# Two of eight query heads multiplied as one product of 512 columns, and the last head's tiles in banks of their own

## The chip, the cores and the metric

The kernel runs on one core of one Trainium2 chip. The metric is device time in microseconds (us) of one execution, the median of several runs. The core's engines are TensorE (PE, with its weight loads listed apart as PEld), VectorE (DVE), ScalarE (ACT), GpSimd (POOL) and SyncE (SP), which here only issues DMAs. Each engine works through its own instructions in order and waits on semaphores for the others.

## What is computed

The reference is two transformer blocks over 256 tokens of width 1024. Each block ends in a "product key" expert layer; the change touches only the first step of that layer, the queries, in both blocks:

```
q = (xb @ w_q).reshape(B, T, PEER_HEADS, 2, PEER_DKEY // 2)     # 8 heads, two halves of 128
s1 = jnp.einsum('bthd,nd->bthn', q[..., 0, :], k1)              # 128 keys for each half
s2 = jnp.einsum('bthd,nd->bthn', q[..., 1, :], k2)
v1, i1 = lax.top_k(s1, PEER_TOPK); v2, i2 = lax.top_k(s2, PEER_TOPK)
...                                                             # 16 of 256 candidates per head,
u_sel = jnp.take(u_tab, idx, axis=0)                            # then the chosen experts
h = jnp.einsum('bthkd,btd->bthk', u_sel, xb)
```

The kernel multiplies by all 16384 experts and masks with gates, rather than gathering.

## The kernel before

**Weights.** All weight matrices pass through one ring of four slots of 128 x 1024 floats. SyncE loads a slot, ScalarE rounds it to `whi` (the type fp32r), and GpSimd (in some stages VectorE) writes the rest `wlo = ring - whi`. The other operand is split in the same way. A product of a weight tile and the operand is then made of three products: `whi` by the rounded operand, `whi` by its rest, `wlo` by the rounded operand. The kernel calls this `split_product` (lines 732 to 734), and each of its matmuls has 256 columns (the 256 tokens).

**The query stage** (function `experts` of each engine, loop over heads `h`). The operand is `R = (rhi, rlo)`, the residual's rounded part and rest. A head has two weight tiles (`c` = 0, 1), one for each half of the query. Function `tile` runs 8 chunks of 128 rows for each, with three matmuls a chunk. Both tiles of a head lie side by side in one PSUM bank, 4 or 5 by turns. The order on TensorE is: the tiles of head `h`, then the scores of head `h - 1` (line 1235), which read the query from `qT`, a buffer of two places in SBUF (`h % 2`). ScalarE copies each head's bank to `qT` when both tiles are done (line 1689, semaphore `q_copied`), then rounds two weight slots (line 1677), then copies the scores of the head before to `scores` (lines 1698 and 1699, semaphore `s_copied`).

**VectorE in this stage.** It first finishes the normed activations in banks 0 to 3 (`normed`), then walks over the heads: `normed_lows` at `h == 1` (line 1941, semaphore `xl_ready`), and for each head and each half of the tokens (`t` = 0, 1) the two levels of `top16` (lines 2252 to 2264, and line 2290 between them). From head 3 on it also adds pairs of expert results: `add_pair`, line 2276, which waits for a copy by ScalarE (line 1705).

**The expert rounds** follow on TensorE: each tile is 8 chunks of one matmul of 512 columns, `whi` by both parts of the normed activations (`hboth`, line 1259), and one of 256 columns, `wlo` by the rounded part (line 1260). Banks 2, 3 and 0, 1 take them. The half of a bank that holds `whi` by the rest is copied out by ScalarE, and VectorE adds the other half.

Of the kernel before, what the change touches and what calls it, by code (L numbers as in the profile page):

```python
# [22 lines left out]
P = 128  # L23
F32 = mybir.dt.float32
F16 = mybir.dt.float16
F32R = mybir.dt.float32r
U32 = mybir.dt.uint32
ALU = mybir.AluOpType
ACT = mybir.ActivationFunctionType
# [3 lines left out]
S = 256  # L33
TT = S // P
KC = D // P
EPS = 1e-6

HEADS = 8
# [10 lines left out]
RING = 4  # L49
# [22 lines left out]
HALF = NKEY // 2  # L72
HALF_ROUND = ROUNDS // 2
U_EXP, U_MID = 12, 13
FIRST_ADD_HEAD = 3
WARM_UP = 9
V_LOGITS = 22
# [44 lines left out]
RAW_AT = 22528  # L122
# [97 lines left out]
def block_program(nc, weights, const1, const2, gains, keys_in, x, out):  # L220
    with ExitStack() as ctx:
# [3 lines left out]
        def over_at(name, base, at, shape, dt=F32):  # L225

            return nc.alloc_sbuf_tensor_at(name, shape, dt, offset=offset_of[base] + at)
# [13 lines left out]
        whi = sb("whi", [P, RING, SLOT], F32R)  # L241
        wlo = sb("wlo", [P, RING, SLOT], F32R)
        act = placed("act", [P, NKEY, S])
# [11 lines left out]
        ps = ctx.enter_context(nc.psum_tensor("ps", [P, 8, 512], F32))  # L255
# [3 lines left out]
        qT = work[:, 2048:3072].rearrange("p (b c t) -> p b c t", b=2, c=2)  # L259
# [55 lines left out]
        start = TT * D  # L315
# [72 lines left out]

        late_scores = carve(LATE_SCORES, 4, TT, 2 * NKEY)[0].rearrange("p b t (c k) -> p b t c k", c=2)

        rhi = over_at("rhi", "act", 4 * RAW_AT, [P, KC, S], F32R)
        rlo = over_at("rlo", "act", 4 * (RAW_AT + KC * S), [P, KC, S], F32R)

        def scores_of(h):

# [18 lines left out]
        lo_ready = [sem(f"lo_ready{j}") for j in range(RING)]  # L414
        left_ready = sem("left_ready")
        sb_left = sem("sb_left_ready")
        slot_used = sem("slot_used")
# [24 lines left out]
        xl_ready = sem("normed_lows_ready")  # L442
# [71 lines left out]
        peer = []  # L514
        for b in (1, 2):
            peer.append({n: sem(f"peer{b}_{n}") for n in (
                "q_copied", "s_ready", "s_copied",
                "gelu_done", "sums_ready", "exp_ready", "sel_ready", "selT_ready", "rows_ready", "eq_ready", "hot_ready",
                "u_low", "u_added", "gates_ready", "gates_used", "shi_ready", "pair_ready", "acc_ready", "done")})
        fin_ready = sem("final_ready")  # L520
# [11 lines left out]
        def bank(i, a=0, b=512):  # L532
            return ps[:, i, a:b]
# [161 lines left out]
        def _(pe):  # L695
# [493 lines left out]
            def experts(b, keys):  # L1189
                n = peer[b]  # L1190
                first_q, first_u, first_v = FIRST[f"q{b + 1}"], FIRST[f"u{b + 1}"], FIRST[f"v{b + 1}"]

                def tile(j, dst, x=(hhi, hlo), kcs=range(KC), start=True):

                    for kc in kcs:
                        c = slice(kc * P, (kc + 1) * P)
                        mm = split_product(dst, (whi[:, j, c], wlo[:, j, c]), (x[0][:, kc, :], x[1][:, kc, :]),
                                           start and kc == 0, kc == KC - 1)
                    if kcs[-1] == KC - 1:
                        mm.then_inc(slot_used, 1)  # L1200

                R = (rhi, rlo)
# [10 lines left out]
                pe.wait_ge(left_ready, left + 4)  # L1213
                for c in range(2):
                    tile(c, bank(4, c * S, (c + 1) * S), R, range(4, 8))
                for h in range(1, HEADS + 1):
                    if h < HEADS:
                        for c in range(2):
                            pe.wait_ge(lo_ready[(2 * h + c) % RING], (first_q + 2 * h + c) // RING + 1)
                            if h >= 2 and c == 0:  # L1220
                                pe.wait_ge(n["q_copied"], h - 1)
                            tile((2 * h + c) % RING, bank(4 + h % 2, c * S, (c + 1) * S), R, range(4 if h + c == 1 else 0, KC))
                            if h + c == 1:
                                scale_turns(2 * b + 1)
                    if h:
                        g = h - 1
                        pe.wait_ge(n["q_copied"], g + 1)
                        if g == 1:
                            pe.wait_ge(xn_ready, 4 * b + 4)
                        if g >= 2:  # L1230
                            pe.wait_ge(n["s_copied"], g - 1)
                        for t in range(TT):
                            for c in range(2):
                                kT = keys[:, c if b == 0 else 2 * g + c, :]
                                mm = pe.matmul(bank(6 + g % 2, (2 * t + c) * P, (2 * t + c + 1) * P),  # L1235
                                               qT[:, g % 2, c, t * P:(t + 1) * P], kT, start=True, stop=True)
                        mm.then_inc(n["s_ready"], 1)
# [44 lines left out]
                for w in range(3):  # L1282
                    for t in range(TT):
                        mm = pe.transpose(bank(4 + w // 2, (w % 2) * S + t * P, (w % 2) * S + (t + 1) * P),
                                          esel[:, t, w, :, :].rearrange("p h k -> p (h k)"), ident[:, :])
# [121 lines left out]
        def _(eng):  # L1407
# [261 lines left out]
            def experts(b):  # L1669
                n = peer[b]  # L1670
# [8 lines left out]
                for h in range(HEADS + 1):  # L1679
                    if h == 2:  # L1680
                        for c in range(4):
                            eng.wait_ge(xn_ready, 4 * b + c + 1)
                            eng.activation(hhi[:, 2 * c:2 * c + 2, :], bank(c).rearrange("p (j t) -> p j t", j=2), ACT.Copy)\
                               .then_inc(xh_ready, 1)
                    if h < HEADS:
                        eng.wait_ge(slot_used, first_q + 2 * h + 2)
                        if h >= 2:
                            eng.wait_ge(n["s_ready"], h - 1)
                        eng.activation(qT[:, h % 2, :, :], bank(4 + h % 2).rearrange("p (c t) -> p c t", c=2), ACT.Copy)\
                           .then_inc(n["q_copied"], 1)  # L1690
                        for c in range(2):
                            high(first_q + 2 * h + c + RING, (2 * h + c) % RING)
                    if h:
                        eng.wait_ge(n["s_ready"], h)
                        if h == 1:
                            eng.wait_ge(nrec, NORM_AT[2 * b + 1] + 1)
                        out = bank(6 + (h - 1) % 2).rearrange("p (t c k) -> p t c k", t=TT, c=2)
                        eng.activation(scores_of(h - 1)[:, 0], out[:, 0], ACT.Copy, scale=token_scale(0))
                        eng.activation(scores_of(h - 1)[:, 1], out[:, 1], ACT.Copy, scale=token_scale(1))\
                           .then_inc(n["s_copied"], 1)  # L1700
# [175 lines left out]
        def _(eng):  # L1876
# [50 lines left out]
            def normed(k):  # L1927

                take_scale(k)
                for b in range(4):  # L1930
                    for c in (2 * b, 2 * b + 1):
                        x = bank(b, c % 2 * S, (c % 2 + 1) * S)
                        last = eng.scalar_tensor_tensor(x, x, gcol[:, k, c:c + 1], scale_row, ALU.mult, ALU.mult)
                    last.then_inc(xn_ready, 1)
# [332 lines left out]
            def experts(b):  # L2267
                n = peer[b]
                first_v = FIRST[f"v{b + 1}"]

                def add_pair(p):

                    eng.wait_ge(n["u_low"], p + 1)
                    bb = BESIDE_BANK[p % 2]
                    a = act[:, 2 * p:2 * p + 2, :]
                    eng.tensor_tensor(a, ps[:, bb:bb + 2, 0:S], a, ALU.add).then_inc(n["u_added"], 1)  # L2276

                normed(2 * b + 1)
                for h in range(HEADS):
                    if h == 1:  # L2280
                        normed_lows(b)
                    eng.wait_ge(n["s_copied"], h + 1)
                    early = 3 * (h - FIRST_ADD_HEAD)
                    for t in range(TT):
                        mid = (lambda: add_pair(early + 1)) if h >= FIRST_ADD_HEAD and t == 1 else None
                        top16([scores_of(h)[:, t, c, :] for c in range(2)], [cand[:, 2, c * NKEY:(c + 1) * NKEY] for c in range(2)],
                              [val[:, c, :] for c in range(2)], [idx[:, t, h, c, :] for c in range(2)], between=mid)

                        s = cand[:, 0, :]
                        last = eng.tensor_tensor(s.rearrange("p (a b) -> p a b", a=TOPK), over(val[:, 0, :], TOPK),  # L2290
                                                 val[:, 1:2, :].to_broadcast([P, TOPK, TOPK]), ALU.add)
                        settle(last)
                        if h >= FIRST_ADD_HEAD and t == 0:
                            add_pair(early)
                        top16([s], [cand[:, 1, :]], [top[:, t, h, :]], [pos[:, t, h, :]])
                        if h >= FIRST_ADD_HEAD and t == 1:
                            add_pair(early + 2)
# [338 lines left out]
```

## Time and profile before

| | |
|---|---|
| median of 3 runs | 1984.44 us (1984.0 to 1984.62) |
| the profiled execution's own time | 1984.3 us |
| its span in the trace | 1982.5 us, 1.8 us less than its time |
| TensorE busy | 1974.8 us, 100% |
| GpSimd, VectorE, ScalarE busy | 1429.7, 1281.9, 1042.3 us |
| mean granted TensorE clock | 0.999 |

Times in rows are microseconds from the span's start unless they are in a column of mean nanoseconds. A matmul's listed duration overlaps with those of its neighbours, since they are pipelined; the distance between two starts is what one of them takes of the engine's time. A "waits" view lists only idle time with what ended it. The chain of work lists, for the work that ended last, each piece on it.

### The profile page before, as it was taken

The numbers are of one execution on the slowest core, as the hardware profiler recorded it, in microseconds if no ns is written. First come the engines' busy times: TensorE is split into PE (matmuls) and PEld (weight loads), VectorE is DVE, ScalarE is ACT, GpSimd is POOL, SyncE is SP. The second block draws the span as 40 slices with busy tenths as digits, with TensorE's granted clock in tenths as the row PEclk, the third lists the DMA queues.
The fourth block names the chain that finished last, engine by engine and source line by source line (L and its number), as shares of the span: only waits on it lengthen the run. The fifth ranks groups of instructions, "written<-read, shape, count | busy, mean of one in ns | idle before, by whom it ended". The sixth has DMA issues, their size and how long they took to land.

```text
span 1982.5 us, 39083 instructions
## 1 busy us (share of the span) xinstructions
PE 1974.8 (100%) x13990; PEld 1766.6 (89%) x13990; DVE 1281.9 (65%) x2178; ACT 1042.3 (53%) x1361; POOL 1429.7 (72%) x606
## 2 busy tenths in 40 slices
PE   9999999999999999999999999999999999999998
PEld 9899898888888888888889899888888888888887
DVE  5256387864766899953336738886467789994333
ACT  6556545565555544445447665556555554444444
POOL 6667878888777878854448757888877787884442
PEclk9999999999999999999999999999999999999999
DMA  8444545555555555566655345555555555555653
GB/s 273 161 139 149 179 161 186 188 183 190 177 170 175 174 169 171 177 208 206 195 186 178 123 144 166 192 187 186 182 176 172 172 178 169 175 174 181 201 190 127
DMA packets 100467, 351.44 MB, mean 177 GB/s; under 512 B 12464, under 2 KB 15408, under 8 KB 100272
## 3 DMA queue, kind: packets, MB, share of 16 engines
q1 hardware_dynamic: 99680, 348.61, 53.2%
q10 hardware_dynamic: 720, 1.92, 0.3%
q8 instruction: 44, 0.72, 0.1%
q14 instruction: 23, 0.19, 0.0%
HBM read 349.44 MB, written 1.05 MB: 177 GB/s over the span
## 4 chain that ended last, share of the span: by engine, by line
PE 99%; DMA 0%; DVE 0%; ACT 0%; POOL 0%; SPq 0%; issue 0%
PE ps L1259 24%; PE ps L1325 12%; PE ps L1260 12%; PE ps L1327 12%; PE ps L1328 6%; PE ps L1326 6%; PE ps L732 4%; PE ps L734 4%; PE ps L733 4%; PE ps L889 4%; PE ps L1251 3%; PE ps L891 2%; PE ps L816 1%; PE ps L1235 1%; PE ps L1137 1%; PE ps L926 1%
## 5 line engine op out<-in xcount | busy, mean ns | idle before, releaser
L653 POOL TENSOR_TENSOR wlo<-ring,whi 128x1024 fp32r<-128x1024 f32 x567 | 1375.2, 2431 | 511.3 <-ACT whi L1677 425.8
L1677 ACT ACTIVATE whi<-ring 128x1024 fp32r<-128x1024 f32 x536 | 566.5, 1060 | 718.2 <-PE ps L1328 387.2
L1259 PE MATMUL ps<-hboth,whi 128*128 128x512 f32 x2048 | 714.6, 395 | 0.0
L1260 PE MATMUL ps<-hboth,wlo 128*128 128x256 f32 x2048 | 567.7, 277 | 0.0
L1259 PEld LDWEIGHTS ps<-hboth,whi 128*128 128x128 f32 x2048 | 384.1, 188 | 87.2
L1325 PE MATMUL ps<-whi,shi 128*128 128x512 f32 x1024 | 404.2, 395 | 0.0
L1327 PE MATMUL ps<-wlo,shi 128*128 128x512 f32 x1024 | 400.4, 391 | 0.0
L1260 PEld LDWEIGHTS ps<-hboth,wlo 128*128 128x128 f32 x2048 | 384.7, 188 | 0.0
L1328 PE MATMUL ps<-whi,slo 128*128 128x256 f32 x1024 | 286.7, 280 | 0.0
L1326 PE MATMUL ps<-whi,slo 128*128 128x256 f32 x1024 | 285.7, 279 | 0.0
L1327 PEld LDWEIGHTS ps<-wlo,shi 128*128 128x128 f32 x1024 | 192.2, 188 | 43.4
L1325 PEld LDWEIGHTS ps<-whi,shi 128*128 128x128 f32 x1024 | 192.4, 188 | 40.3
L2405 DVE TENSOR_TENSOR wlo<-ring,whi 128x1024 fp32r<-128x1024 f32 x64 | 78.7, 1230 | 230.6 <-ACT whi L1677 230.6
L2399 DVE TENSOR_TENSOR slo<-act,shi 128x512 fp32r<-128x512 f32 x128 | 181.9, 1421 | 23.6 <-ACT shi L1739 23.6
L1326 PEld LDWEIGHTS ps<-whi,slo 128*128 128x128 f32 x1024 | 192.3, 188 | 0.0
L1328 PEld LDWEIGHTS ps<-whi,slo 128*128 128x128 f32 x1024 | 192.2, 188 | 0.0
L2358 DVE TENSOR_TENSOR work<-iota,ps 128x1024 f16<-128x1024 f16 x128 | 155.1, 1211 | 0.0
L1446 ACT ACTIVATE whi<-ring 128x1024 fp32r<-128x1024 f32 x105 | 108.0, 1053 | 76.4 <-PE ps L891 35.9
L2368 DVE TENSOR_TENSOR act<-ps,act 128x512 f32 (+1 forms) x128 | 87.0, 682 | 37.9 <-PE ps L1251 32.9
L2276 DVE TENSOR_TENSOR act<-ps,act 128x512 f32<-128x512 f32 x64 | 44.3, 692 | 103.1 <-ACT act L1705 103.0
L2376 DVE TENSOR_TENSOR act<-ps,act 128x512 f32 (+1 forms) x64 | 44.2, 691 | 78.1 <-ACT act L1705 78.1
L732 PE MATMUL ps<-hboth,whi 128*128 128x256 f32 x328 | 94.5, 288 | 0.0
(332 smaller groups left out, 2905.2 us busy)
## 6 DMA issues: line engine op xcount, KB each, us to landing
ring<-in_weights SPq DMA_DIRECT2D x651, 512.0 KB, 3.3
act<-in_const SPq DMA_DIRECT2D x11, 198.0 KB, 4.0
act<-in_const SPq DMA_DIRECT2D x8, 192.0 KB, 4.5
xres<-in_x SPq DMA_DIRECT2D x4, 256.0 KB, 4.9
act<-in_keys ACTq DMA_DIRECT2D x1, 1024.0 KB, 4.7
ring<-in_weights SPq DMA_DIRECT2D x2, 256.0 KB, 4.8
act<-in_fgain ACTq DMA_DIRECT2D x1, 512.0 KB, 3.4
out<-act SPq DMA_DIRECT2D x1, 512.0 KB, 2.6
```

Of the source, the lines that this page charges most:

```text
L653: pool.tensor_tensor(wlo[:, j, :], ring[:, j, :], whi[:, j, :].bitcast(F32), ALU.subtract)\
L732: pe.matmul(dst, wide[0], narrow[0], start=start, stop=False, skip_group_check=True)
L1259: pe.matmul(bank(b), whi[:, j, c], hboth[:, :, kc, :], start=kc == 0, stop=False, skip_group_check=True)
L1260: mm = pe.matmul(bank(b, 0, S), wlo[:, j, c], hhi[:, kc, :], start=False, stop=kc == KC - 1, skip_group_check=True)
L1325: pe.matmul(bank(b), high, whi[:, j, o:o + 512], start=start, stop=False, skip_group_check=True)
L1326: pe.matmul(bank(b, 0, 256), low, whi[:, j, o:o + 256], start=False, stop=stop, skip_group_check=True)
L1327: pe.matmul(bank(b), high, wlo[:, j, o:o + 512], start=False, stop=False, skip_group_check=True)
L1328: return pe.matmul(bank(b, 256, 512), low, whi[:, j, o + 256:o + 512], start=False, stop=stop, skip_group_check=True)
L1446: eng.activation(whi[:, m % RING, :], ring[:, m % RING, :], ACT.Copy).then_inc(hi_ready[m % RING], 1)
L1677: eng.activation(whi[:, j, :], ring[:, j, :], ACT.Copy).then_inc(hi_ready[j], 1)
L2358: eng.tensor_tensor(hot2[:, j], iota[:, :].unsqueeze(1).to_broadcast([P, TOK, NKEY]), over(row(1, at), NKEY), ALU.is_equal)
L2399: eng.tensor_tensor(slo[:, j, :, :], act[:, bass.ds(p * 2, 2), :], shi[:, j, :, :].bitcast(F32), ALU.subtract)\
```

## The change

For heads 5 and 6 a new function `joined_tile` does what the expert rounds do: one matmul of 512 columns, `whi` by `rboth` (which is `rhi` and `rlo` as one tensor at the same addresses), and one of 256 columns, `wlo` by `rhi`. Their banks are 2 and 3 for head 5, and 0 and 1 for head 6 (`JOINED_BANK`). Because those banks hold the normed activations before, TensorE waits for `xl_ready` first. The query now lies in two halves of a bank: ScalarE copies the one to `qT` (semaphore `q_low`), and VectorE adds the other to it (`join_query`, semaphore `q_joined`), at head 2 of its loop, once before each half of the tokens. TensorE's scores of heads 5 and 6 wait for `q_joined`. The last head's two tiles go to banks 5 and 4, half of each, and ScalarE copies each half by itself as soon as its tile is done.

```diff
-        rhi = over_at("rhi", "act", 4 * RAW_AT, [P, KC, S], F32R)
-        rlo = over_at("rlo", "act", 4 * (RAW_AT + KC * S), [P, KC, S], F32R)
+        rboth = over_at("rboth", "act", 4 * RAW_AT, [P, 2, KC, S], F32R)
+        rhi, rlo = rboth[:, 0], rboth[:, 1]
...
+                def joined_tile(j, b):
+
+                    for kc in range(KC):
+                        c = slice(kc * P, (kc + 1) * P)
+                        pe.matmul(bank(b), whi[:, j, c], rboth[:, :, kc, :], start=kc == 0, stop=False, skip_group_check=True)
+                        mm = pe.matmul(bank(b, 0, S), wlo[:, j, c], rhi[:, kc, :], start=False, stop=kc == KC - 1,
+                                       skip_group_check=True)
+                    mm.then_inc(slot_used, 1)
+
+                def query_there(g):
+
+                    if g in JOINED_BANK:
+                        pe.wait_ge(n["q_joined"], list(JOINED_BANK).index(g) + 1)
+                    else:
+                        pe.wait_ge(n["q_copied"], g + 1 if g < min(JOINED_BANK) else g + 1 - len(JOINED_BANK))
+
                 for h in range(1, HEADS + 1):
-                    if h < HEADS:
+                    if h in JOINED_BANK:
+                        pe.wait_ge(xl_ready, 4 * b + 4)
+                        for c in range(2):
+                            pe.wait_ge(lo_ready[(2 * h + c) % RING], (first_q + 2 * h + c) // RING + 1)
+                            joined_tile((2 * h + c) % RING, JOINED_BANK[h] + c)
+                    elif h < HEADS:
...
-                            tile((2 * h + c) % RING, bank(4 + h % 2, c * S, (c + 1) * S), R, range(4 if h + c == 1 else 0, KC))
+                            dst = bank(5 - c, 0, S) if h == HEADS - 1 else bank(4 + h % 2, c * S, (c + 1) * S)
+                            tile((2 * h + c) % RING, dst, R, range(4 if h + c == 1 else 0, KC))
...
-                        pe.wait_ge(n["q_copied"], g + 1)
+                        query_there(g)
...
+                        if h in JOINED_BANK:
+                            eng.activation(qT[:, h % 2, :, :], ps[:, JOINED_BANK[h]:JOINED_BANK[h] + 2, S:2 * S], ACT.Copy)\
+                               .then_inc(n["q_low"], 1)
...
+                        else:
+                            for c in range(2):
+                                eng.wait_ge(slot_used, first_q + 2 * h + c + 1)
+                                last = eng.activation(qT[:, h % 2, c, :], bank(5 - c, 0, S), ACT.Copy)
+                            last.then_inc(n["q_copied"], 1)
...
+                def join_query(h):
+
+                    bb = JOINED_BANK[h]
+                    eng.wait_ge(n["q_low"], list(JOINED_BANK).index(h) + 1)
+                    eng.tensor_tensor(qT[:, h % 2, :, :], ps[:, bb:bb + 2, 0:S], qT[:, h % 2, :, :], ALU.add).then_inc(n["q_joined"], 1)
+
...
+                        if h == 2:
+                            join_query(5 + t)
```

On TensorE, at the border between heads 4 and 5 of the first block, the instructions of the kernel before are these (line 1235 the scores of head 3, then head 5's first tile):

```order
L1235 MATMUL ps<-act,work 128x128 [waits peer1_s_copied,peer1_q_copied]
L1235 MATMUL ps<-act,work 128x128 x3
L732 MATMUL ps<-rhi,whi 128x256 [waits peer1_q_copied,lo_ready2]
L733 MATMUL ps<-rlo,whi 128x256
L734 MATMUL ps<-rhi,wlo 128x256
L732 MATMUL ps<-rhi,whi 128x256
```

At the same place of the changed kernel, with its own line numbers (`normed_lows_ready` is the name of `xl_ready`):

```order
L1259 MATMUL ps<-act,work 128x128 [waits peer1_s_copied,peer1_q_copied]
L1259 MATMUL ps<-act,work 128x128 x3
L1222 MATMUL ps<-rboth,whi 128x512 [waits lo_ready2,normed_lows_ready]
L1223 MATMUL ps<-rboth,wlo 128x256
L1222 MATMUL ps<-rboth,whi 128x512
L1223 MATMUL ps<-rboth,wlo 128x256
```

Two matmuls stand for three, and the first of them waits for VectorE's `normed_lows`. A little further, between heads 6 and 7, the changed kernel has this:

```order
L1223 MATMUL ps<-rboth,wlo 128x256
L1259 MATMUL ps<-act,work 128x128 [waits peer1_s_copied,peer1_q_joined]
L1259 MATMUL ps<-act,work 128x128 x3
L733 MATMUL ps<-rboth,whi 128x256 [waits peer1_q_copied,lo_ready2]
L734 MATMUL ps<-rboth,whi 128x256
```

The scores of head 5 stand behind head 6's tiles as before, but wait for VectorE instead of ScalarE. On VectorE, where head 2 begins in the first block, the kernel before has:

```order
L2264 MAX_INDEX work<-val,work 128x8 [waits dve_step]
L2252 MAX val<-work 128x8 [waits peer1_s_copied,dve_step]
L2252 MAX val<-work 128x8
L2255 MAX_INDEX work<-val,work 128x8 [waits dve_step]
L2256 MATCH_REPLACE work<-val,work 128x128
```

and the changed kernel:

```order
L2298 MAX_INDEX work<-val,work 128x8 [waits dve_step]
L2316 TENSOR_TENSOR work<-ps,work 128x512 [waits peer1_q_low,peer1_s_copied,dve_step]
L2286 MAX val<-work 128x8 x2
L2289 MAX_INDEX work<-val,work 128x8 [waits dve_step]
L2290 MATCH_REPLACE work<-val,work 128x128
```

One addition of 512 elements stands ahead of head 2's first `MAX`; a second one stands ahead of the second half of its tokens.

## Rows read from the trace of the kernel before

**Rows 1.** The profile's page, part 1: busy time of each engine

```profile
PE 1974.8 (100%) x13990; PEld 1766.6 (89%) x13990; DVE 1281.9 (65%) x2178; ACT 1042.3 (53%) x1361; POOL 1429.7 (72%) x606
```

**Rows 2.** Waits of TensorE in the whole span: total us, times, longest

```profile
PE ps L1394 <- DVE work L2466: 1.1, 1, 1.1
PE ps L816 <- DVE wlo L2472: 0.3, 1, 0.3
```

**Rows 3.** Chain of work, first block's query stage: start us, us, what

```profile
284.13 0.89 PE ps L1235 x8
...
290.77 0.89 PE ps L1235 x8
...
297.42 1.85 PE ps L1235 x16
```

**Rows 4.** Windows: length, busy us (instructions) of PE, PEld, DVE, ACT, POOL; clock, DMA, GB/s

```profile
284.13:290.78 6.65, 6.65 (x58) 6.65 (x58) 6.30 (x27) 3.22 (x5) 4.76 (x2) 1.00 0.48 168
305.37:310.91 5.54, 5.54 (x33) 4.84 (x33) 3.63 (x14) 2.61 (x3) 4.98 (x3) 1.00 0.63 204
```

**Rows 5.** Timeline of ScalarE in the expert rounds: start us, us, [idle before]

```profile
313.73 1.06 ACT L1677 ACTIVATE whi<-ring 128x1024 fp32r<-128x1024 f32 x1 [0.62 <-PE ps L1260]
...
413.57 1.06 ACT L1677 ACTIVATE whi<-ring 128x1024 fp32r<-128x1024 f32 x1 [0.71 <-PE ps L1260]
```

**Rows 6.** Timeline of TensorE, query tile: start us, us, line, operands

```profile
285.22 0.28 PE L732 MATMUL ps<-rhi,whi 128*128 128x256 f32 x1
285.33 0.28 PE L733 MATMUL ps<-rlo,whi 128*128 128x256 f32 x1
285.45 0.28 PE L734 MATMUL ps<-rhi,wlo 128*128 128x256 f32 x1
```

**Rows 7.** Timeline of TensorE, expert tile

```profile
305.21 0.39 PE L1259 MATMUL ps<-hboth,whi 128*128 128x512 f32 x1
305.44 0.27 PE L1260 MATMUL ps<-hboth,wlo 128*128 128x256 f32 x1
305.55 0.40 PE L1259 MATMUL ps<-hboth,whi 128*128 128x512 f32 x1
```

**Rows 8.** Timeline of TensorE, output projection with 512 and 256 columns

```profile
224.70 0.40 PE L889 MATMUL ps<-whi,mhi 128*128 128x512 f32 x1
...
235.31 1.03 PE L700 MATMUL ps<-ident,xres 128*128 128x128 f32 x8
```

**Rows 9.** Timeline of ScalarE, copies of heads 5 and 6

```profile
284.17 0.60 ACT L1689 ACTIVATE work<-ps 128x512 f32<-128x512 f32 x1 [3.43 <-PE ps L734]
...
290.81 0.60 ACT L1689 ACTIVATE work<-ps 128x512 f32<-128x512 f32 x1 [3.43 <-PE ps L734]
```

**Rows 10.** Timeline of VectorE, first block: low halves, heads 1 to 3

```profile
273.30 2.48 DVE L1941 TENSOR_TENSOR hboth<-ps,hboth 128x512 fp32r<-128x512 f32 x4
...
278.57 0.43 DVE L2290 TENSOR_TENSOR work<-val 128x256 f32<-128x256 f32 x1
...
287.11 0.49 DVE L2252 MAX8 val<-work 128x8 f32<-128x128 f32 x2
...
293.24 0.49 DVE L2252 MAX8 val<-work 128x8 f32<-128x128 f32 x2
...
302.76 1.37 DVE L2290 TENSOR_TENSOR work<-val 128x256 f32<-128x256 f32 x1
307.11 0.69 DVE L2276 TENSOR_TENSOR act<-ps,act 128x512 f32<-128x512 f32 x1 [2.97 <-ACT act L1705]
```

**Rows 11.** Timeline of VectorE, second block: head 2's second half, first add

```profile
1226.08 0.49 DVE L2252 MAX8 val<-work 128x8 f32<-128x128 f32 x2
...
1239.94 0.69 DVE L2276 TENSOR_TENSOR act<-ps,act 128x512 f32<-128x512 f32 x1 [2.96 <-ACT act L1705]
```

**Rows 12.** Chain of work, second block's last scores

```profile
1230.25 1.85 PE ps L1235 x16
```

**Rows 13.** Timeline of GpSimd, one head's cycle

```profile
285.79 4.76 POOL L653 TENSOR_TENSOR wlo<-ring,whi 128x1024 fp32r<-128x1024 f32 x2 [1.88 <-ACT whi L1677]
```

More of the change, by code:

```diff
@@ L74 @@
 U_EXP, U_MID = 12, 13
+JOINED_BANK = {5: 2, 6: 0}
 FIRST_ADD_HEAD = 3
@@ L516, in block_program @@
             peer.append({n: sem(f"peer{b}_{n}") for n in (
-                "q_copied", "s_ready", "s_copied",
+                "q_copied", "q_low", "q_joined", "s_ready", "s_copied",
                 "gelu_done", "sums_ready", "exp_ready", "sel_ready", "selT_ready", "rows_ready", "eq_ready", "hot_ready",
@@ L1220, in experts @@
                             if h >= 2 and c == 0:
-                                pe.wait_ge(n["q_copied"], h - 1)
-                            tile((2 * h + c) % RING, bank(4 + h % 2, c * S, (c + 1) * S), R, range(4 if h + c == 1 else 0, KC))
+                                pe.wait_ge(n["q_copied"], h - 1 if h < HEADS - 1 else min(JOINED_BANK))
+                            dst = bank(5 - c, 0, S) if h == HEADS - 1 else bank(4 + h % 2, c * S, (c + 1) * S)
+                            tile((2 * h + c) % RING, dst, R, range(4 if h + c == 1 else 0, KC))
                             if h + c == 1:
@@ L1685, in experts @@
                     if h < HEADS:
-                        eng.wait_ge(slot_used, first_q + 2 * h + 2)
+                        if h < HEADS - 1:
+                            eng.wait_ge(slot_used, first_q + 2 * h + 2)
                         if h >= 2:
                             eng.wait_ge(n["s_ready"], h - 1)
-                        eng.activation(qT[:, h % 2, :, :], bank(4 + h % 2).rearrange("p (c t) -> p c t", c=2), ACT.Copy)\
-                           .then_inc(n["q_copied"], 1)
+                        if h in JOINED_BANK:
+                            eng.activation(qT[:, h % 2, :, :], ps[:, JOINED_BANK[h]:JOINED_BANK[h] + 2, S:2 * S], ACT.Copy)\
+                               .then_inc(n["q_low"], 1)
+                        elif h < HEADS - 1:
+                            eng.activation(qT[:, h % 2, :, :], bank(4 + h % 2).rearrange("p (c t) -> p c t", c=2), ACT.Copy)\
+                               .then_inc(n["q_copied"], 1)
+                        else:
[3 more added lines that the diff above has]
+                            last.then_inc(n["q_copied"], 1)
                         for c in range(2):
```

## The prediction

> **What bounds the kernel now.** I read the page's busy times first: TensorE is busy 1974.8 of 1982.5 us, the next engine 1429.7 [rows 1]. A share of the whole span can hide waits, so I asked for TensorE's waits. There are two in the whole execution, 1.1 and 0.3 us, both near the start and neither in the stage of the change [rows 2]. The chain of work says the same of the query stages: one piece of TensorE follows another, with nothing between [rows 3, 12]. So each nanosecond that TensorE's own stream gets shorter there comes off the end, and a wait put before it is paid in full.
>
> The question is then what TensorE's stream costs. Listed durations can't be summed: a query tile's matmuls are listed with 0.28 us, but start 0.11 to 0.12 us apart [rows 6]. The reader should use distances between starts.
>
> **The cost of a tile, old form.** The scores of two neighbouring heads start at 284.13, 290.77 and 297.42: a head takes 6.645 us, of which its scores take 0.89 [rows 3]. The rest is two tiles, 2.878 us each; with 24 matmuls a tile that is 119.9 ns a matmul and 360 ns a chunk.
>
> **The cost of a tile, new form.** The expert rounds already run exactly the new pair, 512 columns of `whi` by both parts and 256 of `wlo`. Two of ScalarE's roundings, each released by a tile's end, stand at 313.73 and 413.57, with 36 tiles between [rows 5]: 2.773 us a tile, 347 ns a chunk. The timeline shows how: the 512 start takes 0.23 us, the 256 start 0.11 to 0.12 [rows 7]. Columns streamed stay at 768 a chunk; what goes is about 13 ns for each matmul left out.
>
> **TensorE's sum.** Two heads of two tiles in each of two blocks are 8 tiles: 8 x (2.878 - 2.773) = 0.84 us less. The operand and the place differ from the expert rounds, so I bound the new pair. In the output projection, pairs of 512 and 256 columns go from 224.70 to 235.31, 30 of them [rows 8]: 354 ns each, 6 ns less than the old chunk, or 0.4 us less in 64 chunks. On the other side, the last two heads' scores together take 1.85 us, not twice 0.89 [rows 3, 12]. Should that 0.07 be the wait for the last head's copy, the split copy could give 2 x 0.07 back, so the gain is 0.4 to 1.0 us. I take 0.84, since those rows have the same shapes, the same order and the same weight slots. I take nothing for the split copy: ScalarE's copy takes 0.60 us [rows 9], and the scores of head 6 cover it with their 0.89.
>
> A sentence on the notes: the Trainium skill, page "TensorE: Matmul & The Clock Gate", section "Wait — 56ns, not 53.3ns?", puts a fixed cost of about 2.5 ns on each matmul beyond its columns. By that, 64 fewer would give an estimated 0.16 us, against 0.84 from the rows. The rows show 12 to 13 ns a matmul, and the measurement decides.
>
> **The waits that are added, in TensorE's time.** Each is checked for how early its releaser is.
> - Head 5 waits for `xl_ready`. The low halves start at 273.30 and take 2.48, ending 275.8 [rows 10]. Head 5 begins one head and the scores before 284.13 + 0.89: at 285.02 - 6.645 = 278.4. That is 2.6 us early. Head 6 asks for nothing more.
> - Head 5's scores wait for the first join, where they stood at 290.77 [rows 3]; with four shorter tiles they come at 290.35. ScalarE's copy begins at 284.17 and takes 0.60 [rows 9], so it is done at 284.8 or earlier. VectorE comes to head 2 at 287.11 and so finds it done. An addition of this shape out of PSUM takes 0.69 [rows 10]; it ends at 287.8, 2.5 us early.
> - Head 6's scores wait for the second join, at 297.42 - 0.42 = 297.0. ScalarE's part is done by 291.4 [rows 9]. VectorE's second half of head 2 stood at 293.24 and is one join later, 293.93; this join ends at 294.6, 2.4 us early. In the second block the same numbers are 1226.08 + 2 x 0.69 = 1227.5 against 1230.25 - 0.42 = 1229.8, 2.4 us early [rows 11, 12].
>
> **VectorE's extra work**, two joins of 0.69 a block, is 1.4 us. What is queued behind them is heads 2 to 7, and then the first `add_pair`, for which TensorE's later rounds wait. Before that first addition VectorE sits idle 2.97 us in the first block and 2.96 in the second, waiting for ScalarE [rows 10, 11]. The 1.4 us go in there, and even with ScalarE's release 0.4 us sooner some 1.1 us of idle time is left. If that cover were gone, the rest would be carried down the queue, and TensorE has more slack in its banks before it waits. So: nothing.
>
> **ScalarE, GpSimd and the loads.** ScalarE's copies for heads 5 and 6 are as long as before; for the last head one of 512 columns becomes two of 256, the first in time in which it sat 3.43 us idle each head [rows 9]. GpSimd splits a head's two tiles in 4.76 us and then idles 1.88 [rows 13]; a head 0.21 shorter leaves 1.67. DMA is busy 0.48 in a head's cycle and 0.63 in the expert rounds, which run at the new pace already [rows 4]. Nothing.
>
> **Sum.** 1984.3 - 0.84 = 1983.5 by the profiled execution, which was 0.14 under the median of the three runs. By the median it is 1983.6, my forecast.
>
> **The rivals.**
> - *The gain is lost in the columns.* What is streamed is the same 768 columns; the pace of the output projection's pairs, or one still nearer the old chunk, leaves 0 to 0.4 us: about 1984.3. For it: those 354 ns [rows 8]. Against: the same shapes in the expert rounds.
> - *Weight loads set the pace.* In the head's cycle the load unit is busy 6.65 of 6.65 us, in the expert rounds 4.84 of 5.54 [rows 4]. If a load and not the columns filled each slot, leaving 64 out would save 64 x 120 ns = 7.7 us: 1976.7, faster by 0.4%. Against: a 512-column matmul would then start its follower after 0.12 us, and it does so after 0.23 [rows 7]. The Trainium skill, page "TensorE: Matmul & The Clock Gate", section "Back-to-back issue gap", lets load and matmul set the distance together and gives 131 ns for 512 columns; no such short distance is in these rows. Chance 2 in 100.
> - *A join comes late.* TensorE stands still while VectorE is in its top-16 work. The addition between its two levels takes 0.43 to 1.37 us from one half to another [rows 10]; were five of them ahead of the second join 0.65 longer each, that join would be 3.25 later, 0.8 beyond the slack of 2.4, in each block. That is 1984.44 - 0.84 + 1.6 = 1985.2. It decides, slower than before, from 2.4 + 0.42 = 2.8 us of lateness in each block, and passes 0.2% (4 us, about the least that a measurement of this kernel can tell from no change) from 4.8 us. For it: VectorE is 6.30 of 6.65 us busy there [rows 4]. Against: both blocks show the same slack.
>
> **How the numbers follow.** The forecast has 0.80 (its own range 1983.0 to 1984.2), the lost gain 0.11, weight loads 0.02, a late join 0.05, of which 0.02 is beyond 0.2%; 0.02 is left for what I don't see, on both sides. The range goes from the full 1.0 us off the lowest runs (1984.0 - 1.0 = 1983.0) less 0.4 for their scatter, 1982.6, up to the late join, 1985.2. Faster by over 0.2%: 0.03; slower: 0.03; within: 0.94.
>
> **What would show it.** Right: new tiles 2.77 us apart, the two heads' cycles 6.44 instead of 6.645, 64 matmuls fewer, TensorE's waits still two; VectorE idle before its first `add_pair` shrunk from 2.97 to about 1.1. Wrong: a wait of TensorE's scores for VectorE's join, or of head 5's first matmul for the low halves; new tiles at 2.88; or head cycles near 5 us.

## The result, and the profile after

The changed kernel takes 1988.97 us in the median of 13 runs (1988.47 to 1990.29), against 1984.45 us of the kernel before (13 runs): a ratio of 1.0023, 95% interval 1.0016 to 1.0031. That is 4.5 us slower, where 0.84 us faster was forecast. Its profiled execution took 1989.01 us with a span of 1987.2, 4.7 us over the span before. Two single executions on record stand far outside all others and count in no ratio: 3255 us of the kernel before (beside e1 to e4) and 6940 us of e2; nothing on record says why.

I first checked the stage that the change touches. The chain of work of the changed kernel, at the places of [rows 3] (line 1259 is the scores, 1235 before):

```profile
277.44 0.89 PE ps L1259 x8
...
283.98 0.89 PE ps L1259 x8
...
290.42 0.89 PE ps L1259 x8
...
297.06 1.78 PE ps L1259 x16
```

Head 5 takes 6.54 us and head 6 takes 6.44, against 6.645. The last scores take 1.78 instead of 1.85. Together that is 0.38 us a block, 0.76 in both, close to the forecast. The trace has 64 matmuls fewer, 13926 against 13990, as forecast. TensorE's waits, the whole answer, answer to [rows 2]: none was added.

```profile
PE ps L1418 <- DVE work L2508: 1.1, 1, 1.1
PE ps L817 <- DVE wlo L2514: 0.4, 1, 0.4
```

VectorE's timeline has the two joins (line 2316) and then the first `add_pair` (line 2310), which answers to the last row of [rows 10]:

```profile
287.07 0.69 DVE L2316 TENSOR_TENSOR work<-ps,work 128x512 f32<-128x512 f32 x1
...
293.37 0.69 DVE L2316 TENSOR_TENSOR work<-ps,work 128x512 f32<-128x512 f32 x1
...
306.79 0.69 DVE L2310 TENSOR_TENSOR act<-ps,act 128x512 f32<-128x512 f32 x1 [3.24 <-ACT act L1739]
```

The joins are on time, and VectorE still idles 3.24 us before its first addition. That is not the 1.1 us that was forecast: the two joins did go into its queue, but its own additions between the two levels of `top16` were shorter by more than that. Of three such additions from 289 us on, the kernel before has 0.85, 1.37 and 1.37 us, the changed one 0.42, 0.42 and 0.99. The second of them, before and after:

```profile
296.12 1.37 DVE L2290 TENSOR_TENSOR work<-val 128x256 f32<-128x256 f32 x1
```

```profile
296.84 0.42 DVE L2332 TENSOR_TENSOR work<-val 128x256 f32<-128x256 f32 x1
```

Why their length varies no run here shows. The query stage did what was asked of it. The loss is behind it, in code that the change doesn't touch. ScalarE's roundings in the expert rounds, each released by a tile's end, answer to [rows 5]:

```profile
313.56 1.06 ACT L1701 ACTIVATE whi<-ring 128x1024 fp32r<-128x1024 f32 x1 [0.68 <-PE ps L1284]
...
415.32 1.06 ACT L1701 ACTIVATE whi<-ring 128x1024 fp32r<-128x1024 f32 x1 [0.77 <-PE ps L1284]
```

Again 36 tiles lie between, but they take 2.827 us each instead of 2.773. TensorE's timeline of such a tile shows where, beside [rows 7] (1283 and 1284 are the lines 1259 and 1260 before):

```profile
305.11 0.28 PE L1284 MATMUL ps<-hboth,wlo 128*128 128x256 f32 x1
305.23 0.40 PE L1283 MATMUL ps<-hboth,whi 128*128 128x512 f32 x1
305.47 0.28 PE L1284 MATMUL ps<-hboth,wlo 128*128 128x256 f32 x1
305.59 0.40 PE L1283 MATMUL ps<-hboth,whi 128*128 128x512 f32 x1
305.83 0.28 PE L1284 MATMUL ps<-hboth,wlo 128*128 128x256 f32 x1
305.94 0.40 PE L1283 MATMUL ps<-hboth,whi 128*128 128x512 f32 x1
306.17 0.28 PE L1284 MATMUL ps<-hboth,wlo 128*128 128x256 f32 x1
306.29 0.40 PE L1283 MATMUL ps<-hboth,whi 128*128 128x512 f32 x1
```

Three chunks go from 305.23 to 306.29, 353 ns each. In the kernel before, two chunks go from 305.21 to this row, 693 ns by the unrounded starts, 347 each:

```profile
305.90 0.39 PE L1259 MATMUL ps<-hboth,whi 128*128 128x512 f32 x1
```

Nobody waits; the same instructions are simply spaced a little wider. How long this lasts is best seen by counting instructions in windows of equal length. First the kernel before, then the changed one; the first number behind the window is its length, the next TensorE's busy time with its matmuls in brackets, then that of its weight loads:

```profile
320.00:431.00 111.00, 111.00 (x642) 97.10 (x641) 91.97 (x245) 62.59 (x81) 96.53 (x41) 1.00 0.57 189
450.00:475.00 25.00, 25.00 (x146) 22.05 (x145) 9.30 (x13) 14.57 (x19) 21.75 (x10) 1.00 0.58 191
500.00:620.00 120.00, 120.00 (x955) 105.13 (x954) 83.87 (x119) 61.92 (x80) 95.09 (x41) 1.00 0.52 173
1260.00:1371.00 111.00, 111.00 (x642) 97.01 (x641) 90.43 (x233) 64.55 (x83) 95.21 (x40) 1.00 0.58 189
```

```profile
320.00:431.00 111.00, 111.00 (x630) 96.30 (x629) 90.13 (x242) 61.22 (x80) 94.12 (x40) 1.00 0.55 184
450.00:475.00 25.00, 25.00 (x147) 21.86 (x146) 8.61 (x12) 13.61 (x18) 21.95 (x10) 1.00 0.61 198
500.00:620.00 120.00, 120.00 (x954) 105.09 (x953) 84.39 (x119) 61.53 (x80) 96.28 (x40) 1.00 0.52 174
1260.00:1371.00 111.00, 111.00 (x630) 96.22 (x629) 90.70 (x235) 61.16 (x78) 94.47 (x40) 1.00 0.56 187
```

The slower pace fills rounds 0 to 12 of both blocks (642 against 630 matmuls) and is gone behind them, where the program has six transposes of the gate rows between the tiles. The granted clock is 1.00 in all of these windows. The 52 tiles cost 52 x (2.827 - 2.773) = 2.8 us more a block, 5.6 in both. With the 0.76 gained this makes +4.8 us, and the span grew by 4.7.

In what follows, "fast pace" is 347 ns a chunk of one 512- and one 256-column matmul, "slow pace" 353 to 354.

### The profile page after: what moved, and what is told of

It is laid out like the page before. It is cut to its first block, busy times and chain, and to the rows that moved or that the text cites. A ratio compares the mean times of both kernels' runs of the same rounds, so it can differ in the third digit from the quotient of the medians.

```text
span 1987.2 us, 38963 instructions
## 1 busy us (share of the span) xinstructions
PE 1979.4 (100%) x13926; PEld 1766.0 (89%) x13926; DVE 1281.1 (64%) x2182; ACT 1042.6 (52%) x1363; POOL 1428.7 (72%) x606
## 4 chain that ended last, share of the span: by engine, by line
PE 99%; DMA 0%; DVE 0%; ACT 0%; POOL 0%; SPq 0%; issue 0%
PE ps L1283 24%; PE ps L1284 12%; PE ps L1349 12%; PE ps L1351 12%; PE ps L1352 6%; PE ps L1350 6%; PE ps L733 4%; PE ps L735 4%; PE ps L734 4%; PE ps L890 4%; PE ps L1275 3%; PE ps L892 2%; PE ps L817 1%; PE ps L1222 1%; PE ps L1259 1%; PE ps L1138 1%
```

## The experiments

What differs where the rounds begin is small. In the kernel before, the last two heads' scores take 1.85 us in the chain [rows 3, 12]: TensorE waits for ScalarE's copy of the last head, and one distance between starts is 175 ns instead of 112. In the changed kernel the split copy is there in time and the wait is gone. My theory was that this "lost wait" had set the pace; the rival was that the joined heads or their banks did.

**e1: the changed kernel with one copy.** The last head as before, heads 5 and 6 joined.

```diff
-                            dst = bank(5 - c, 0, S) if h == HEADS - 1 else bank(4 + h % 2, c * S, (c + 1) * S)
+                            dst = bank(4 + h % 2, c * S, (c + 1) * S)
...
-                            for c in range(2):
-                                eng.wait_ge(slot_used, first_q + 2 * h + c + 1)
-                                last = eng.activation(qT[:, h % 2, c, :], bank(5 - c, 0, S), ACT.Copy)
...
```

> The changed kernel with the last head as before: both tiles in one bank, one copy by ScalarE. Heads 5 and 6 stay joined. In the changed kernel's trace the first 13 expert rounds of each block (52 tiles) run at 353.6 ns a chunk against 346.7 before, 2 x 52 x 8 x 6.9 ns = 5.7 us, and the short wait in the last two heads' scores (a 9th start 175 ns behind the 8th, against 112) is gone. Theory 'lost wait': that wait put TensorE's stream into the fast pace. Here it is back, the rounds run at 346.7 again, and the kernel takes 1984.45 - 0.6 = 1983.8 us. Rival 'joined heads': the new products or their banks set the slow pace, and the kernel stays at about 1989.1 us.

1984.15 us, ratio 1.0002 (0.9992 to 1.0011). Its chain has the wait again, and its first window the old count:

```profile
297.04 1.85 PE ps L1259 x16
```

```profile
320.00:431.00 111.00, 111.00 (x642) 97.02 (x641) 91.97 (x243) 62.54 (x80) 96.49 (x41) 1.00 0.56 189
```

The joined heads alone don't make the slow pace. The 0.35 us over the expected 1983.8 may come from a short slow stretch: in the profiled execution, of 1984.36 us, rounds 13 to 15 of the second block and the first tile of round 16 ran at 353 ns, 13 tiles or 0.7 us. One of its ten executions took 1988.48 us; I return to this at e13.

**e2: the kernel before with the last head split only.** The same lines the other way round, no joined heads, and one more wait so that bank 4 is free for the second tile.

```diff
+                            if h == HEADS - 1 and c == 1:
+                                pe.wait_ge(n["q_copied"], h)
+                            dst = bank(5 - c, 0, S) if h == HEADS - 1 else bank(4 + h % 2, c * S, (c + 1) * S)
...
+                            for c in range(2):
+                                eng.wait_ge(slot_used, first_q + 2 * h + c + 1)
+                                last = eng.activation(qT[:, h % 2, c, :], bank(5 - c, 0, S), ACT.Copy)
...
```

> The kernel before with only the last head changed: its two tiles in banks 5 and 4, copied one by one; no joined heads. Theory 'lost wait': the scores' wait goes, the 52 tiles run at 353.6 ns a chunk, and the kernel takes 1984.45 + 5.7 - 0.14 = 1990.0 us. Rival 'joined heads': nothing changes the pace, 1984.3 us.

1989.72 us in the median of 8 runs, ratio 1.0027 (1.0016 to 1.0038): the whole loss, from the part of the change for which I had booked nothing.

```profile
297.14 1.78 PE ps L1238 x16
```

```profile
320.00:431.00 111.00, 111.00 (x630) 96.19 (x629) 90.18 (x242) 61.23 (x80) 94.11 (x41) 1.00 0.54 184
```

**e3: two banks, both copies late.**

```diff
-                                eng.wait_ge(slot_used, first_q + 2 * h + c + 1)
+                                eng.wait_ge(slot_used, first_q + 2 * h + 2)
```

> The changed kernel, but ScalarE's two copies of the last head both wait for the second tile; the banks stay 5 and 4. The second copy then ends about 0.66 us after the tile, against 0.60 for the one copy before. Theory 'lost wait': TensorE's scores wait again, somewhat over 63 ns, and the pace is fast: 1983.9 us. If any wait does it, that holds whatever its length; if the length matters (a phase), the pace can stay slow. Rival 'banks of the last head': slow, 1989 us.

1984.14 us, 0.9999 (0.9989 to 1.0009). The scores take 1.97 us, so the wait is about three times as long, and the pace is fast. The banks of the last head are not the cause. Nor is the layout of TensorE's program: its instructions are those of the changed kernel to the last one, and only ScalarE's copy comes later.

**e4: 18 small matmuls instead of 16.** Between the scores and the first expert tile stand 16 fp16 matmuls of 64 columns, whose results nobody reads; two more shift that tile by 60 ns without any wait.

```diff
-                for _ in range(2 * TOK):
+                for _ in range(2 * TOK + 2):
```

> The changed kernel with 18 instead of 16 small fp16 matmuls between the scores and the first expert tile (30 ns each, together 60 ns, as long as the lost wait). If the slow pace is a matter of when the first expert matmul starts in some rhythm, shifting it by 60 ns gives the fast pace back, 1983.9 us. If it takes an empty queue, a wait, to reset, the pace stays slow: 1989.1 us.

1983.77 us, 0.9998 (0.9988 to 1.0008), 642 matmuls in the first window. So the wait as such is not needed either. What counts is when, or in what state, the stream is entered; I call an entry the place where the expert tiles' matmuls begin or go on behind something else. "Lost wait" was half a theory: it fits this change and fails as a rule.

**e5, e6: 17 and 20 of them.** The same line with + 1 and + 4.

> The changed kernel with 17 small fp16 matmuls ahead of the first expert tile instead of 16; with 18 the fast pace was back. Theory 'rhythm': the pace hangs on when the first expert matmul starts within some rhythm, and 30 ns later is a third place in it; either pace is possible, 1984.0 or 1989.0 us, and nothing between. Rival 'load ahead': more time for the weight loads to run ahead is what helps, and 17 lie between 16 (slow) and 18 (fast).

> The changed kernel with 20 small fp16 matmuls. Theory 'rhythm': 120 ns later than with 16; the pace may be slow again, 1989.2 us, if the rhythm has come round. Rival 'load ahead' (more time ahead of the first expert tile helps): fast as with 18, 1984.0 us. A slow pace here would rule the rival out; a fast one leaves both open.

1983.42 us (0.9997, 0.9987 to 1.0006) and 1983.71 us (0.9997, 0.9988 to 1.0007), both fast. They left the rival "more time ahead is what helps" open.

**e7: the kernel before with 18.** The line of e4 in the kernel before.

> The kernel before, with 18 small fp16 matmuls instead of 16: its wait of 63 ns in the last scores and 60 ns of dummies on top. Theory 'rhythm': this is a further place, 123 ns behind the slow one; the same answer as with 20 dummies in the changed kernel. 1984.5 us if fast, 1990 us if slow. Rival 'any delay resets': fast.

1989.05 us, 1.0025 (1.0015 to 1.0035). This was a surprise in its place. The windows:

```profile
320.00:431.00 111.00, 111.00 (x642) 97.88 (x641) 91.97 (x245) 62.60 (x81) 96.61 (x41) 1.00 0.56 189
450.00:475.00 25.00, 25.00 (x143) 21.69 (x142) 9.06 (x13) 14.54 (x19) 21.18 (x10) 1.00 0.58 190
500.00:620.00 120.00, 120.00 (x942) 104.31 (x941) 83.07 (x118) 60.42 (x77) 94.02 (x40) 1.00 0.50 169
```

Rounds 0 to 12 are fast. The pace turns slow at the next entry, behind the transposes, nearly 150 us after the two added matmuls, and stays so through the rounds with gates (942 matmuls against 955). So a shift of 60 ns can decide the pace at a later entry. Something of it can be seen already before that entry: with the same 642 matmuls in the first window, the weight loads are busy 97.88 us instead of the 97.10 of the kernel before. I return to this behind e12.

**e8: a break after the first round.** 16 more such matmuls, into bank 4, between round 0 and the loop of the changed kernel.

```diff
                 beside_round(0, first=True)
+                for _ in range(2 * TOK):
+                    pe.matmul(bank(4, 0, HALF), iota[:, :], iota[:, 0:HALF], start=True, stop=True)
                 with pe.Fori(1, U_MID) as k:
```

> The changed kernel with 16 further small fp16 matmuls (into bank 4) after the first expert round, ahead of the loop. Theory 'the pace, once taken, lasts until the stream is broken': the four tiles of round 0 stay slow (353.6 ns a chunk), and the break gives a new draw; if it is fast, 48 tiles in each block run at 346.7 and the kernel takes 1989.0 - 2 x 48 x 8 x 0.0069 + 2 x 0.5 for the dummies = 1984.7 us. Rival 'the slow pace comes from something in these rounds other than how they are entered' (VectorE's or ScalarE's work beside them, the joined banks): the rounds stay slow, 1990 us.

1984.96 us, 1.0004 (0.9995 to 1.0014), 0.3 from what was expected. The first window has 643 matmuls; only round 0 stays slow:

```profile
320.00:431.00 111.00, 111.00 (x643) 97.10 (x642) 91.98 (x246) 62.59 (x81) 96.54 (x41) 1.00 0.56 190
```

This shows that a break can end the slow pace, and that what runs beside these rounds (VectorE, ScalarE, the loads) doesn't by itself keep it up.

**e9 to e12: 15, 14, 12 and 1 of them.** The line of e4 with - 1, - 2, - 4 and - 15, in the changed kernel.

> The changed kernel with 15 small fp16 matmuls ahead of the first expert tile. So far 16 without a wait is slow and everything with more time ahead of that tile (17, 18, 20 matmuls, or a wait of 63 ns or more) is fast in the 52 tiles. Theory 'rhythm': the entry hits one of a few places, so less time ahead can be fast as well; with 15, 14, 12 and 1 at least one of the four should be, 1983.7 us. Rival 'load ahead': too little time is what makes them slow, so 15 and fewer are all slow, 1989 us.

> The changed kernel with 14 small fp16 matmuls, 59 ns less ahead of the first expert tile. 'Rhythm': fast or slow, 1983.6 or 1989 us. 'Load ahead': slow, 1989 us.

> The changed kernel with 12 small fp16 matmuls, 117 ns less. 'Rhythm': fast or slow, 1983.5 or 1989 us. 'Load ahead': slow, 1989 us.

> The changed kernel with a single small fp16 matmul ahead of the first expert tile, 436 ns less. 'Rhythm': fast or slow, 1983.1 or 1988.6 us. 'Load ahead': slow, 1988.6 us. If 15, 14, 12 are fast and this one is slow, a number of small matmuls is needed to break the rhythm of what went before.

| kernel, small matmuls | us (median) | ratio to before, 95% | slow tiles in the profiled execution |
|---|---|---|---|
| changed, 15 (e9) | 1992.87 (4 runs) | 1.0043 (1.0027 to 1.0060) | 180: first block rounds 0 to 31, second 0 to 12 |
| changed, 14 (e10) | 1987.94 | 1.0020 (1.0010 to 1.0029) | 89: first block rounds 13 to 31, second 13 to the first tile of 16 |
| changed, 12 (e11) | 1983.39 | 0.9995 (0.9986 to 1.0005) | none |
| changed, 1 (e12) | 1982.48 | 0.9992 (0.9982 to 1.0001) | none |

The last column is from distances between 512-column starts in the trace (353 ns against 347). The slow tiles account for the times. With 0.054 us for each, and 0.029 us for each small matmul in each block, e9 should be 1983.5 - 0.1 + 9.7 = 1993.1 us and e10 1983.5 - 0.1 + 4.8 = 1988.2, within 0.3 of what was measured; 1983.5 is about what e4, e5 and e6 leave for 16 at the fast pace. The changed kernel itself has 104 slow tiles, which gives 1989.1 us. 12 and 1 are fast with less time ahead than the slow 16, so "more time ahead" falls. The windows of e9, the slowest kernel here, are slow in all four places:

```profile
320.00:431.00 111.00, 111.00 (x630) 96.19 (x629) 90.06 (x241) 61.22 (x80) 94.34 (x40) 1.00 0.55 184
450.00:475.00 25.00, 25.00 (x143) 21.68 (x143) 8.60 (x12) 13.23 (x17) 21.35 (x10) 1.00 0.58 188
500.00:620.00 120.00, 120.00 (x941) 104.20 (x941) 81.70 (x117) 61.88 (x80) 93.45 (x39) 1.00 0.51 170
1260.00:1371.00 111.00, 111.00 (x630) 96.32 (x629) 90.13 (x238) 61.47 (x79) 94.46 (x40) 1.00 0.56 187
```

**What precedes a slow entry behind the transposes.** The 16 traces, two blocks each, have 32 stretches of rounds 0 to 12. The fast ones come in two kinds, told apart by the weight loads' busy time in the window. The second block of e7 and that of e1 are of the rarer kind:

```profile
1260.00:1371.00 111.00, 111.00 (x642) 97.88 (x641) 91.82 (x237) 62.60 (x81) 96.60 (x41) 1.00 0.56 189
```

```profile
1260.00:1371.00 111.00, 111.00 (x642) 97.86 (x641) 89.89 (x228) 64.97 (x83) 94.54 (x40) 1.00 0.56 189
```

Five stretches have 97.86 to 97.88 us (both blocks of e7 and e10, the second of e1), and all five are slow behind the transposes. Nineteen have 96.99 to 97.10, and none of them is. Of the eight slow stretches one stays slow there, the first of e9. So an entry is hardly a fresh draw: what it brings went with the pattern in which the stream ran before. This was read from the traces afterwards, and no run was made to test it.

A break doesn't always end the slow pace either. From round 16 on, 32 small matmuls for the gates stand in each round. In the first block of e7, e9 and e10 the slow pace went on across all 16 of these breaks, and in the second block of e1, e7 and e10 it ended at the first.

**e13, e14: one small matmul in both kernels, side by side.**

> The kernel before with a single small fp16 matmul ahead of the first expert tile instead of 16: 2 x 0.44 us of dummies less. If all expert rounds run at 346.7 ns a chunk: 1984.3 - 0.9 = 1983.4 us. If this entry falls on the slow pace somewhere, 3 to 9 us more, and then it tells nothing of the change's own gain.

> The changed kernel with a single small fp16 matmul, as e12, beside e13 on the same chip. Theory 'the local sum was right': 0.8 us under e13 where both run at the fast pace throughout, 1982.5 us, and 1.7 us under the kernel before, outside its interval. Rival 'no gain of its own': the same as e13, 1983.4 us.

e13: 1983.20 us (0.9994, 0.9985 to 1.0003); e14: 1982.61 us (0.9992, 0.9982 to 1.0001). The difference, 0.6 us, is near the 0.8 expected, but neither interval excludes 1 against the kernel before, though e14's was expected to. e14 is the same kernel as e12; the two have the lowest medians of all, and it is the version I would keep. That it beats the kernel before is shown only by its medians, 1.7 us lower twice, of which 0.9 are the small matmuls left out.

e13 shows one more thing. Ten of its eleven executions took 1982.9 to 1983.6 us, and the profiled one 1989.28. The trace of that one has rounds 0 to 12 of both blocks at the slow pace:

```profile
320.00:431.00 111.00, 111.00 (x630) 96.31 (x629) 90.44 (x244) 61.23 (x79) 94.04 (x41) 1.00 0.56 185
```

The ten others weren't traced, but the gap of 6.1 us is near the 5.6 of 104 tiles. So with TensorE's short wait for ScalarE still in it, one program can fall on either pace from one execution to the next. e1's one execution of 1988.48 us may be another such case; it wasn't traced. That being profiled brought on the slow pace of e13 isn't ruled out by a run, but in no other kernel does the profiled execution stand apart from the rest. e13 also shows that the wait doesn't ensure the fast pace.

## Why the prediction was wrong

- **What bounds the kernel** was right: TensorE is busy throughout in both kernels, and the view of waits has the same two. But that view is not proof of a stream without waits. The 63 ns for which the kernel before waits in each block's last scores (175 ns between two starts instead of 112) are not in it, and only the chain's 1.85 gave them away.
- **The tile's cost, query stage.** Forecast 0.84 us in all. The trace has 0.38 a block: 0.105 in head 5, 0.205 in head 6 and 0.07 in the last scores. So the tiles gave 0.62 us in both blocks and not 0.84, and that the sum comes so near the forecast is partly luck: 0.14 of it is the wait for which nothing was booked. Head 5 itself runs at the slow pace (2.83 us a tile) and head 6 mostly at the fast one, so that two of the rows by which I bounded the new pair, 354 [rows 8] and 347 [rows 5], are the two paces and not a small and a large estimate of one. At equal pace e5, with its one small matmul more, was 0.75 us under the kernel before of its own runs, and e14 was 0.6 under e13.
- **The added waits and VectorE's extra work** cost nothing, as forecast. The joins run at 287.07 and 293.37. The rival "a join comes late" didn't happen. The sign "idle shrunk from 2.97 to about 1.1" failed: it was 3.24, since VectorE's additions between the two levels were 1.8 us shorter in all. Those are the additions whose length that rival was about; they varied in the other direction.
- **The rivals** were all placed inside the query stage. None had a mechanism that acts behind it, so none was near 1989.
- **The step that failed** is the one on the sum's reach: "So each nanosecond that TensorE's own stream gets shorter there comes off the end." I took 2.773 us a tile as a property of the expert rounds' instructions. It is a property of those instructions and of how the stream was entered. The term that should have stood in the sum is 104 tiles at 0 or +0.054 us each, 0 or 5.6 us (e9 shows that it can be 180 tiles); I know no row of the kernel before that tells which.
- **"I take nothing for the split copy."** The reason given, that head 6's scores of 0.89 us cover the copy's 0.60, was wrong: the 63 ns of waiting were there in spite of it. They vanished with the split copy, 0.07 us a block, as my bound had it. But that vanished wait moved the entry: e2, with this part alone, has the whole loss, and e1, without it, has none.

## What to carry to other kernels

Where one engine is busy for the whole span, its spacing itself has to be checked before and after: count its instructions in equal windows in code that didn't change. Two rows that disagree by 2% on the same shapes are a finding, not an error bar. A change of tens of nanoseconds ahead of a long, evenly spaced stream can be worth several microseconds either way, so a small local change is best judged with a few variants that shift the entry, and not by one build.

## What the runs showed of the hardware

- A stream of alternating 512- and 256-column matmuls on TensorE, each with its weight load, had two steady spacings at the same granted clock of 1.00: 347 ns a pair and 353. The slow one repeats every three pairs (starts 113, 233, 117, 241, 120 and 236 ns apart). The fast one comes in two patterns: one repeats every two pairs (112, 233, 117 and 231), the other every pair (116 to 117 and 230). The all-256 stream of the query stage had one spacing, 120 ns.
- In rounds 0 to 12 a spacing once taken held for all 52 tiles, 147 us at the slow pace, through loop iterations and semaphore checks that are met. It changed only at a break: six transposes, 16 small fp16 matmuls (e8) or the 32 of the gates. Not every break changed it.
- Shifts of 30 to 60 ns ahead of the first entry changed its pace. The first expert matmul was followed after 318 to 319 ns in the changed kernel, e2 and e8, which are slow there, and after 312 to 315 in all the others; but of those e9 and e13 were slow too. At the transposes the pattern before them went with the pace behind them, as told above. What state it is that differs stays open: the rows give the spacings and not what the array and its weight loads do inside them.
- Three rows are alike, or nearly so, at the two paces, and so explain nothing: the granted clock (1.00 in both), the listed weight loads (187 to 190 ns in both for all but some 50 in the window) and the DMA share in the first window (0.57 and 0.55). The Trainium skill, page "TensorE: Matmul & The Clock Gate", section "Wait — 56ns, not 53.3ns?", gives one spacing for each number of columns, about 2.5 ns over the columns' own time; these runs have 230 to 241 ns for 512 columns with alternating weight loads, and differ among themselves by more than that 2.5. The measurement decides.
